# The last layer norm of a MoE layer on one Trainium2 core: tiles centred two places behind their gating, the last residual ahead of two centrings

## The reference

```
xp = _layer_norm(ALPHA * xp + gf * _hier_moe(xp * (1 + cf) + sf, *moe_params), ln2_g[l], ln2_b[l])
xs = _layer_norm(ALPHA * xs + gf * _hier_moe(xs * (1 + cf) + sf, *moe_params), ln2_g[l], ln2_b[l])

def _layer_norm(x, g, b):
    mu = mean(x); var = mean((x - mu)**2)
    return (x - mu) * rsqrt(var + 1e-5) * g + b
```

## Time and profile before

| | us |
|---|---|
| median of 3 runs (551.97 to 552.78) | 552.16 |
| profiled execution, span from first to last instruction | 550.5 |
| PE busy | 509.6 (93%) |
| DVE busy | 437.4 (79%) |
| ACT busy | 273.5 (50%) |
| POOL busy | 98.9 (18%) |

### The profile page before, as it was taken

The page is one execution under the profiler, slowest core; times in us unless marked ns, Lnnn a source line. Parts: engine busy times, 40 slices in busy tenths (PEclk is TensorE's granted clock), DMA queues, the critical chain, the costliest instruction groups (busy, mean ns, idle before and its releaser), DMA issues.

```text
span 550.5 us, 8091 instructions
## 1 busy us (share of the span) xinstructions
PE 509.6 (93%) x3137; PEld 421.5 (77%) x3138; DVE 437.4 (79%) x703; ACT 273.5 (50%) x378; POOL 98.9 (18%) x114
## 2 busy tenths in 40 slices
PE   4999999999999997999999999999999999998670
PEld 1579999997799995777787788877888888886220
DVE  3217899989798803998559879989999999996984
ACT  2336412002031313997712224767888888884373
POOL 0005800003000001232000000212624242312201
PEclk9999999999999999999999999999999999999786
DMA  8997995729876551228188209989999999998667
GB/s 298 387 386 242 232 349 184 240 79 279 320 245 233 173 134 41 59 60 230 41 298 340 89 39 338 422 321 397 387 391 388 375 384 370 375 310 311 252 190 157
DMA packets 56831, 142.36 MB, mean 259 GB/s; under 512 B 8375, under 2 KB 17138, under 8 KB 50904
## 3 DMA queue, kind: packets, MB, share of 16 engines
q1 hardware_dynamic: 44792, 119.06, 60.3%
q0 software_dynamic: 9120, 20.80, 12.9%
q10 hardware_dynamic: 2880, 1.98, 1.2%
HBM read 129.71 MB, written 20.20 MB: 272 GB/s over the span
## 4 chain that ended last, share of the span: by engine, by line
PE 64%; DVE 18%; issue 7%; DMA 5%; ACT 3%; SPq 1%; DVEq 0%; POOL 0%; ACTq 0%; POOLq 0%
PE PS L1861 9%; PE PS L1863 9%; PE PS L1862 9%; PE PS L1959 8%; PE PS L1960 8%; PE PS L1964 8%; DVE PS L1391 2%; DMA uni<-in_w_ada 2%; PE PS L2266 2%; DMA g<-x_rows 2%; DVE w_lo L1525 2%; PE PS L2380 2%; DVE uni L1407 2%; ACT uni L948 1%; PE PS L2194 1%
## 5 line engine op out<-in xcount | busy, mean ns | idle before, releaser
L1861 PE MATMUL PS<-w_hi,act_hi 128*128 128x512 f32 x244 | 98.7, 405 | 0.9 <-DVE act_lo L1619 0.9
L1959 PE MATMUL PS<-act_hi,w_hi 128*128 128x320 f32 x320 | 97.6, 313 | 0.2 <-issue 0.2
L1960 PE MATMUL PS<-act_lo,w_hi 128*128 128x320 f32 x320 | 96.3, 309 | 0.0
L1863 PE MATMUL PS<-w_hi,act_lo 128*128 128x512 f32 x244 | 95.4, 391 | 0.0
L1862 PE MATMUL PS<-w_lo,act_hi 128*128 128x512 f32 x244 | 95.2, 390 | 0.0
L1281 DVE SCALAR_TENSOR_TENSOR uni<-raw,uni 128x512 f32<-128x512 f32 x112 | 75.1, 743 | 0.0
L1964 PE MATMUL PS<-act_hi,w_lo 128*128 128x320 f32 x320 | 72.9, 309 | 0.0
L1959 PEld LDWEIGHTS PS<-act_hi,w_hi 128*128 128x128 f32 x320 | 60.1, 188 | 4.2 <-issue 3.2
L1960 PEld LDWEIGHTS PS<-act_lo,w_hi 128*128 128x128 f32 x320 | 60.1, 188 | 0.0
L803 ACT ACTIVATE w_hi<-raw 128x2048 fp32r<-128x2048 f32 x14 | 26.4, 1915 | 58.5 <-PE PS L1964 48.3
L1861 PEld LDWEIGHTS PS<-w_hi,act_hi 128*128 128x128 f32 x244 | 45.9, 188 | 11.8 <-issue 1.9
(11 more groups left out here) (285 smaller groups left out, 934.2 us busy)
## 6 DMA issues: line engine op xcount, KB each, us to landing
raw<-in_w_ada SPq DMA_DIRECT2D x20, 1024.0 KB, 7.6
raw<-in_w_expert_in SPq DMA_DIRECT2D x16, 1024.0 KB, 11.8
uni<-in_w_expert_out SPq DMA_DIRECT2D x15, 1024.0 KB, 11.1
raw<-in_w_in SPq DMA_DIRECT2D x12, 1024.0 KB, 8.3
g<-in_w_expert_in SPq DMA_DIRECT2D x8, 1024.0 KB, 12.0
uni<-expert_rows SPq DMA_DIRECT2D x10, 512.0 KB, 7.2
uni<-in_w_ada SPq DMA_DIRECT2D x4, 1024.0 KB, 14.5
raw<-in_w_out SPq DMA_DIRECT2D x4, 1024.0 KB, 6.2
```

Source lines behind the costliest of these rows:

```text
L1861: T.matmul(out, lh, rh, start=first, stop=False)
L1863: return T.matmul(out, ll, rh, start=False, stop=last)
L1959: T.matmul(out, a, h_hi[:, k, sl], start=f, stop=False)
L1960: T.matmul(out, a, h_lo[:, k, sl], start=False, stop=False)
```

## The change

VectorE centres place n - 2, not n - 1, and does so between the mean of n and the add of n + 1 (for n = 2 and 3); places 2 and 3 are centred behind the last residual, which is drawn ahead of them. ScalarE scales place n - 2 behind the deviation of n, and place 3 behind all others, behind squares and deviation of place 4 too. The deviation and its reciprocal have one column for each place.

```diff
@@ views
+        fin_std = small[:, 93:93 + NT]
+        fin_rstd = small[:, 32:32 + NT]
@@ scalar
             def scaled_rows(n):
                 act.wait_ge(s_fu, n + 1)
                 u = fin_y[:, n, 1, :]
-                b = (NT + n) % 2
-                nc.scalar.activation(u, u, ACT.Copy, scale=rstd[:, b:b + 1]).then_inc(s_fin, 1)
+                nc.scalar.activation(u, u, ACT.Copy, scale=fin_rstd[:, n:n + 1]).then_inc(s_fin, 1)
...
-                b = (NT + n) % 2
-                nc.scalar.activation(std[:, b:b + 1], sq_sum[:, n:n + 1], ACT.Sqrt, bias=eps, scale=1.0 / D).then_inc(s_std, 1)
+                nc.scalar.activation(fin_std[:, n:n + 1], sq_sum[:, n:n + 1], ACT.Sqrt, bias=eps, scale=1.0 / D).then_inc(s_std, 1)
...
             for n in range(NT):
-                if n == NT - 1:
-                    scaled_rows(n - 1)
                 squares(n)
                 deviation(n)
                 if n + 3 < NT:
                     weight_rows(n + 3)
-                if 1 <= n < NT - 1:
-                    scaled_rows(n - 1)
+                if n >= 2:
+                    scaled_rows(n - 2)
+            scaled_rows(NT - 2)
@@ vector
+            def final_inverse(n):
+                dve.wait_ge(s_std, NT + n + 1)
+                link(V.reciprocal(fin_rstd[:, n:n + 1], fin_std[:, n:n + 1]))
+
+            def last_residual():
+                n = NT - 1
+                u, z = fin_y[:, n, 0, :], fin_y[:, n, 1, :]
+                dve.wait_ge(s_fm, NT)
+                dve.wait_ge(s_fz, NT - 1)
+                V.scalar_tensor_tensor(out=z, in0=x1[:, T_ORDER[n], :], scalar=ALPHA, in1=u, op0=ALU.mult, op1=ALU.add).then_inc(s_fz, 1)
...
             def last_tile():
                 n = NT - 1
-                b = (NT + n) % 2
                 u, z = fin_y[:, n, 0, :], fin_y[:, n, 1, :]
-                V.scalar_tensor_tensor(out=z, in0=x1[:, T_ORDER[n], :], scalar=ALPHA, in1=u, op0=ALU.mult, op1=ALU.add).then_inc(s_fz, 1)
                 dve.wait_ge(s_fz, NT)
                 link(V.scalar_tensor_tensor(out=u, in0=z, scalar=neg_mean[:, n:n + 1], in1=fin_v[:, 2, :], op0=ALU.add, op1=ALU.mult))
-                inverse(NT + n)
+                final_inverse(n)
...
-            for n in range(NT + 1):
-                if n < NT:
-                    gate_rows(n)
-                    mean(n)
+            for n in range(NT):
+                gate_rows(n)
+                mean(n)
+                if 2 <= n < NT - 1:
+                    final_inverse(n - 2)
+                    centred(n - 2)
                 if n + 1 < NT:
                     add_rows(n + 1)
-                if 1 <= n < NT:
-                    inverse(NT + n - 1)
-                    centred(n - 1)
+            last_residual()
+            for n in (NT - 3, NT - 2):
+                final_inverse(n)
+                centred(n)
             last_tile()
```

More of the change, by code:

```diff
@@ L1813, in centred @@
                                        op0=ALU.add, op1=ALU.mult).then_inc(s_fu, 1)
+            def final_inverse(n):
[7 more added lines that the diff above has]
+                V.scalar_tensor_tensor(out=z, in0=x1[:, T_ORDER[n], :], scalar=ALPHA, in1=u, op0=ALU.mult, op1=ALU.add).then_inc(s_fz, 1)
             def last_tile():
                 n = NT - 1
-                b = (NT + n) % 2
                 u, z = fin_y[:, n, 0, :], fin_y[:, n, 1, :]
-                V.scalar_tensor_tensor(out=z, in0=x1[:, T_ORDER[n], :], scalar=ALPHA, in1=u, op0=ALU.mult, op1=ALU.add).then_inc(s_fz, 1)
                 dve.wait_ge(s_fz, NT)
                 link(V.scalar_tensor_tensor(out=u, in0=z, scalar=neg_mean[:, n:n + 1], in1=fin_v[:, 2, :], op0=ALU.add, op1=ALU.mult))
-                inverse(NT + n)
+                final_inverse(n)
                 for h in range(2):
                     c = slice(h * CH, (h + 1) * CH)
-                    V.scalar_tensor_tensor(out=u[:, c], in0=u[:, c], scalar=rstd[:, b:b + 1], in1=fin_v[:, 3, c], op0=ALU.mult,
+                    V.scalar_tensor_tensor(out=u[:, c], in0=u[:, c], scalar=fin_rstd[:, n:n + 1], in1=fin_v[:, 3, c], op0=ALU.mult,
                                            op1=ALU.add).then_inc(s_finl, 1)
```

## The result

The changed kernel takes 554.77 us in the median of 22 runs (552.62 to 556.56), the kernel before 551.99 us in the median of 22. The ratio is 1.0044, with a 95% interval of 1.0032 to 1.0056: 2.4 us slower (2.8 us by the medians), where I had forecast 0.4 us and a range that ended at 553.5. The profiled execution was one of the fastest of the 22 (552.76 us, span 551.0), and in it nearly all of the forecast schedule is found.

What follows compares the result with a forecast made beforehand. The prediction saw DVE bounding the kernel ahead of a closing drain of POOL's stores and SP's halves. Store 2's delay added 0.4 us to the 550.5 span; with 1.66 us from span to median, 552.5 us, range 551.0 to 553.5.

Steps and rivals of the forecast that it cites:

- (e): POOL's stores: store 1 issued at 536.2, store 2 at 539.6 (0.63 us later), store 3 at 540.95 (was 540.90).
- the sum behind it: End of the program: store 2 lands -0.2 to +0.6 us later, taken as +0.4, same amounts behind it; span 550.9.
- the halves follow: End of the drain: after POOL's stores of tiles 2 and 3, SP's halves land last, at about 548.7.
- Whether the halves slip in before store 3 or behind it, the sum of the bytes is the same: Drain at the end: the order of store 3 and SP's halves was taken not to matter.
- (a) to (c): VectorE's centring order, last residual drawn ahead, last deviation: DVE's part ends 1.7 us earlier.
- the stall of 1.88 us: DVE's wait for ScalarE's first deviation, 525.37 to 527.25 in the trace of before; forecast to shrink to 0.41 us.
- Rival 2: TensorE's clock falls before gated sum 3, delaying POOL's stores: +1.0 to +1.4 us, 553.2 to 553.6; chance 0.20.
- the spacings of DVE: VectorE's schedule rebuilt from traced spacings, such as add to its gating 1.32 us and gating to mean 1.27.
- the wait that went: DVE's wait for ScalarE's deviation at the last centring, 0.43 us before; forecast to go.
- the one that shrank: DVE's wait at the first centring, forecast to shrink from 1.88 to 0.41 us.
- the last residual's wait that costs nothing: On DVE, the last residual's new wait for gated sum 3 costs nothing, at full or half clock.
- rival 1: End: halves don't wait behind the stores, the end moves with DVE; gain 1.2 us at most, 551.0; chance 0.20.

Runs made afterwards that it cites:

- b_look2: The kernel before, unchanged, traced again: gated sums 2 and 3 at 1.98 us each, end 29.9 us behind the first add.
- a_warm: The changed kernel plus two unused 512-column matmuls on TensorE between the gated sums of places 2 and 3: 553.62 us, ratio 1.0035 to before.
- a_look3: The changed kernel, no edit, traced again: gated sum 3 at full clock, end 32.4 us behind the first add.
- a_dve_only_warm: The changed kernel with ScalarE's old order, VectorE's new one, and two filler matmuls before gated sum 3: 553.89 us, ratio 1.0042 to before.
- b_look4: The kernel before, unchanged, traced again: gated sums 2 and 3 took 3.56 and 1.98 us, end 30.1 us behind the first add.
- a_again: The changed kernel, no edit, run and traced again: 555.56 us, ratio 1.0058 to before.
- best: The changed kernel with centring 2 and scaling 2 earlier, two filler matmuls, place 3 scaled by VectorE and stored plainly by SP: 549.62 us, ratio 0.9962 to before.
- b_plain: The kernel before with POOL's four last-layer-norm stores plain, not accumulating (bias of four tiles left out): 549.52 us, ratio 0.9945.

## Why the prediction was wrong

**The step that failed** is (e) with the sum behind it: "store 2 at 539.6 (was 538.97): 0.63 us later". 539.6 was met (539.45). "Was 538.97" was one execution's number, and an unusual one: measured from the first add, before has store 2 at 18.6 to 19.1 us in three of four further traces, and the changed kernel has it at 20.3 to 21.2. The term is 1.4 us (18.9 to 20.3, b_look2 against a_warm, both at full clock), not 0.63 with a sum of 0.4. Where the first gated sum is late in both kernels, 0.63 was nearly right (0.55, a_look3 against the first trace). But when that sum is early, as in the four further traces of before, the old order lets store 2 go 1.1 to 1.7 us sooner where gated sum 3 is at full clock (18.6 to 19.1 against 20.3), and the changed order only 0.5 us (20.3 against 20.8).

**The end** was read from the wrong store. That "the halves follow" is true, but the span hangs on POOL's last store plus 3.06 us. From the wrong reading came the sentence "Whether the halves slip in before store 3 or behind it, the sum of the bytes is the same". The bytes are, but the cost isn't: behind store 3 the halves are free, ahead of it they put off the landing that counts. The spacing of stores 2 and 3 grew by 0.6 us (3.2 against 2.6), and that is the halves' doing: with the halves late it is 2.6 again, though the two stores are issued as close together (a_dve_only_warm). 1.4 + 0.6 is nearly the 2.1 us between a_warm and b_look2 at full clock; the interval of a_warm, 1.0 to 2.8 us, holds it.

**VectorE's gain** in (a) to (c), 1.7 us, came for the most part from the stall of 1.88 us, which is 0 to 0.28 in the four further traces of before. The first half is computed 22.1 to 22.7 us behind the first add in b_look2 to b_look4 and at 21.5 to 22.1 in the changed kernel: a gain of about 0.7 us by the means, and none of it reaches the end.

**Rival 2**, given 0.20, named a second mechanism that is real: the half clock in the gated sum of place 3 was found in two of three traces of the changed kernel (3.68 and, partly, 2.69). Where it lasts through the sum it costs 1.6 us (a_again against a_warm), a little over the 1.0 to 1.4 that I had worked out. But it isn't the main term, for 1.0035 stays when the clock is held. How large its share in the median is was not settled: it showed in the medians of one pair of runs out of three. Among all traces without the two matmuls, gated sum 3 is slow in 5 of 7 with VectorE's new order and in 2 of 8 with its old one.

Right were the spacings of DVE, the wait that went and the one that shrank (it is 0.42 us or nothing), the last residual's wait that costs nothing, store 2 as the one whose delay reaches the end, and rival 1's rejection: the 1.7 us didn't pass through. That the span of the first pair grew by the 0.4 us of the forecast was luck, as said above. The columns were not tested by themselves.

## What to carry to other kernels

Ask which landing the program's close waits for, and look at the row of the rendezvous: a wait that shrinks by what another grows shows that neither is the end. When a transfer is not the last one needed, issuing it earlier can hurt, because it takes turns on the DMA engines with the one that is. Take the base of a forecast of 1 us from several executions, measured from a common point close by; one trace here was off by 1.6 to 1.9 us against three of four others, in just the stretch that was changed.

## What was not expected of the hardware

- POOL's closing instruction ends 2.8 us behind the landing of POOL's last store, and the program 3.02 to 3.06 us, in all 17 traces with accumulating stores. In best the program ends only 0.5 us behind the landing of SP's last half. One trace shows this, so it is a hint and no more that a last store is better issued on SP.
- A 512 KB accumulating store of POOL takes 5.0 to 5.3 us to its mean landing when alone (store of place 0, 17 traces), and one that queues behind another lands 2.5 to 2.7 us behind it when nothing gets in between. A plain one takes 2.8 us (b_plain).
- TensorE's granted clock fell to 0.53 in the gated sum that followed 2.06 us of idling (a_again), and stayed at 1.00 after 2.22 us (a_look3) and 2.28 us (b_look2): in these traces the length of the pause alone doesn't say whether it falls.
